# Hybrid decoder layer: block sums moved from GpSimd to VectorE, squares added by accumulating DMAs, embedding projection rounded in the last pair

## The reference

```python
h = h + y @ w_out[i]
hn = rmsnorm(h, ffn_norm_g[i])                     # D_MODEL 2048, D_FF 5632
h = h + (silu(hn @ w_gate[i]) * (hn @ w_up[i])) @ w_down[i]
e = rmsnorm(p[i] @ ple_proj[i], ple_norm_g[i])     # p: 512 x 256
gate = sigmoid(rmsnorm(h, ple_gate_norm_g[i]) @ ple_gate_w[i] + ple_gate_b[i])
h = h + gate * e
```

## Time and profile before

| | us |
|---|---|
| runs: median of 3 (lowest, highest) | 2752.56 (2748.27, 2755.18) |
| the profiled execution, its own time | 2750.89 |
| its span, first to last instruction | 2749.2 |
| PE busy | 2642.3 (96%) |
| DVE busy | 1756.5 (64%) |
| ACT busy | 1137.2 (41%) |
| POOL busy | 804.4 (29%) |

### The profile page before, as it was taken

The page is one execution under the profiler, slowest core; times in us unless marked ns, Lnnn a source line. Parts: engine busy times, 40 slices in busy tenths (PEclk is TensorE's granted clock), DMA queues, the critical chain, the costliest instruction groups (busy, mean ns, idle before and its releaser), DMA issues.

```text
span 2749.2 us, 49201 instructions
## 1 busy us (share of the span) xinstructions
PE 2642.3 (96%) x18730; PEld 2250.5 (82%) x18730; DVE 1756.5 (64%) x2078; ACT 1137.2 (41%) x1690; POOL 804.4 (29%) x672
## 2 busy tenths in 40 slices
PE   7999999999999998799999999999979999999998
PEld 6776776776776787799999999999977888888887
DVE  6654653653653535799999999999974333334443
ACT  5445535534534425444444444444433222223321
POOL 3101200210111105755555555555534000001100
PEclk9999999999999999899999999999999999999999
DMA  5222231232232334343343343344347453533532
GB/s 168 87 77 64 70 86 59 69 86 66 65 90 93 128 95 137 104 134 116 121 141 120 115 140 127 114 137 130 114 171 267 128 179 101 176 95 99 178 122 72
DMA packets 126526, 319.11 MB, mean 116 GB/s; under 512 B 37272, under 2 KB 39832, under 8 KB 126392
## 3 DMA queue, kind: packets, MB, share of 16 engines
q1 hardware_dynamic: 108096, 251.30, 29.5%
q0 software_dynamic: 18304, 66.07, 6.4%
HBM read 276.88 MB, written 40.44 MB: 115 GB/s over the span
## 4 chain that ended last, share of the span: by engine, by line
PE 37%; issue 33%; DVE 20%; POOL 5%; ACT 3%; DMA 2%; SPq 1%; DVEq 0%; POOLq 0%; ACTq 0%
PE bank L349 11%; PE bank L346 11%; PE bank L350 11%; DVE w_lo L1323 10%; DVE act_out_lo L1397 3%; DVE u_s L1417 2%; PE bank L387 1%; POOL probs L1128 1%; DVE cu L1393 1%; DVE w_lo L341 1%; DMA raw<-w_mix 1%; POOL scratch_pool L140 1%; PE bank L1355 1%; DVE cg L1412 1%; PE bank L1357 1%
## 5 line engine op out<-in xcount | busy, mean ns | idle before, releaser
L341 DVE TENSOR_TENSOR w_lo<-raw,w_hi 128x1024 fp32r<-128x1024 f32 (+2 forms) x308 | 331.5, 1079 | 424.6 <-ACT w_hi L334 423.2
L334 ACT ACTIVATE w_hi<-raw 128x1024 fp32r<-128x1024 f32 (+2 forms) x308 | 284.8, 926 | 517.1 <-PE bank L350 412.3
L346 PE MATMUL bank<-in_hi,w_hi 128*128 128x512 f32 x1088 | 457.7, 421 | 37.8 <-DVE in_lo L2002 11.4
L349 PE MATMUL bank<-in_lo,w_hi 128*128 128x512 f32 x1088 | 442.7, 407 | 0.0
L350 PE MATMUL bank<-in_hi,w_lo 128*128 128x512 f32 x1088 | 429.6, 395 | 0.0
L1355 PE MATMUL bank<-x_a,w_hi 128*128 128x256 f32 x1408 | 405.1, 288 | 24.1 <-DVE cu L1421 14.5
L1356 PE MATMUL bank<-x_a,w_hi 128*128 128x256 f32 x1408 | 400.0, 284 | 0.0
L1357 PE MATMUL bank<-x_a,w_lo 128*128 128x256 f32 x1408 | 400.0, 284 | 0.0
L1323 DVE TENSOR_TENSOR w_lo<-sum,w_hi 128x1024 fp32r<-128x1024 f32 x176 | 308.3, 1752 | 6.4 <-ACT w_hi L1318 6.3
L1355 PE MATMUL bank<-x_c,w_hi 128*128 128x256 f32 x1056 | 300.4, 284 | 7.1 <-DVE x_c L1267 4.5
L1356 PE MATMUL bank<-x_c,w_hi 128*128 128x256 f32 x1056 | 299.9, 284 | 0.0
(11 more groups left out here) (290 smaller groups left out, 5091.6 us busy)
## 6 DMA issues: line engine op xcount, KB each, us to landing
raw<-w_gu SPq DMA_DIRECT2D x154, 512.0 KB, 5.0
raw<-w_mix SPq DMA_DIRECT2D x116, 512.0 KB, 3.7
raw<-w_down SPq DMA_DIRECT2D x64, 384.0 KB, 3.1
raw<-w_down SPq DMA_DIRECT2D x64, 320.0 KB, 2.9
raw<-ple_gate SPq DMA_DIRECT2D x32, 512.0 KB, 3.6
raw_odd<-w_gu SPq DMA_DIRECT2D x22, 512.0 KB, 5.8
act_scratch<-act_out_hi POOLq DMA_DIRECT2D x44, 256.0 KB, 3.8
act_scratch<-act_out_lo POOLq DMA_DIRECT2D x44, 256.0 KB, 4.0
```

Of the source, the lines that this page charges most:

```text
L334: nc.scalar.activation(w_hi[:, ring_slots(par2, half), 0:cols[half]], raw[:, half, 0:cols[half]], ACT.Copy).then_inc(hi_ready, 1)
L341: nc.vector.tensor_tensor(w_lo[:, s, 0:cols[half]], raw[:, half, 0:cols[half]], w_hi[:, s, 0:cols[half]].bitcast(F32), ALU.subtract).then_ ...
L346: nc.tensor.matmul(out, w_h, x_hi, start=start, stop=False, skip_group_check=True)
L349: nc.tensor.matmul(out, w_h, x_lo, start=False, stop=False, skip_group_check=True)
```

## The change

The sums of weight blocks and of activation blocks are formed by DVE (`dve_sum`, `dve_x_sums`) and no longer by POOL. `hf` has three buffers in turn. The squares of the late output projection go to two buffers by parity and from there to DRAM by POOL DMAs, which after the first two add to what lies there (`accum_op`); at the end two DMAs bring the two sums back, and PE adds both in `norm_bank` before product 3 of the first pair. The fourth activation sum is cut within the first pair (`act_x6`, `dve_x6`). In the last pair ACT and DVE cut the embedding `p` and the four halves of `ple_proj` in their slots after product 3. `sq_e` has four buffers.

```diff
+    hf = [sb_at(first + k * KB, f"hf_{i}", [P, SEQ]) for i, k in enumerate((64, 154, 156))]
+    sq_h = [sb_at(first + k * KB, f"sq_h_{i}", [P, SEQ]) for i, k in enumerate((162, 164))]
...
+    def squares_added(o):
+        return S(f"moved_{o % 2}"), 16 + 16 * (o // 2 + 1)
+
+    def act_late_square(act, o):
+        if o > 1:
+            act.wait_ge(*squares_added(o - 2))
+        nc.scalar.activation(sq_h[o % 2][:], h_t[:, o, :], ACT.Square).then_inc(S("h_squared"), 1)
+
+    def pool_late_square(pool, o):
+        pool.wait_ge(S("h_squared"), o + 1)
+        if o > 1:
+            pool.wait_ge(*squares_added(o - 2))
+            pool.dma_start(squares_dram[o % 2], sq_h[o % 2][:], accum_op=ALU.add).then_inc(S(f"moved_{o % 2}"), 16)
...
     def act_x_scaled(act, o):
-        i = o // 2
         act.wait_ge(*added_late(o))
-        if i > 0:
-            act.wait_ge(S("x_summed_pool"), KT // 2 + 4 * i)
-            act.wait_ge(S("hn_ready"), 3 * i - 1)
+        if o > 2:
+            act.wait_ge(S("x_summed_dve"), KT // 2 + 4 * ((o - 1) // 2))
+            act.wait_ge(S("hn_ready"), 3 * ((o - 3) // 2) + 2)
...
     def dve_x_sums(dve, i):
+        nc.vector.tensor_tensor(t123[:, 0, :], b12, b11, ALU.subtract).then_inc(S("x_summed_dve"), 1)
+        nc.vector.tensor_tensor(t123[:, 2, :], b22, b12, ALU.subtract).then_inc(S("x_summed_dve"), 1)
+        dve.wait_ge(S("x_summed_dve"), summed(1))
+        nc.vector.tensor_tensor(t123[:, 1, :], b22, t123[:, 0, :], ALU.subtract).then_inc(S("x_summed_dve"), 1)
+        dve.wait_ge(S("x_summed_dve"), summed(3))
+        nc.vector.tensor_tensor(t4[:, i, :], b21, t123[:, 1, :], ALU.subtract).then_inc(S("x_summed_dve"), 1)
...
@@ pe_pair
-            if first and j == 2:
-                pe.wait_ge(S("h_summed"), KT + 1)
-                nc.tensor.matmul(aux[:], ones[:], acc_h[:], start=True, stop=True, skip_group_check=True
-                                 ).then_inc(S("norm_summed"), 1)
+            if first and j == 3:
+                for half in range(2):
+                    pe.wait_ge(S(f"moved_{half}"), SQUARES_BACK)
+                    last = nc.tensor.matmul(norm_bank[:], ones[:], sq_h[half][:], start=half == 0, stop=half == 1,
+                                            skip_group_check=True)
+                last.then_inc(S("norm_summed"), 1)
@@ act_pair
+            if first and j == 1:
+                act_x6(act)
+            if first and j == 3:
+                rstd_of(act, rstd_h, NORM_FFN, norm_bank)
...
+            if last and j == 3:
+                for k in range(2):
+                    nc.scalar.activation(p_hi[:, k, :], p_raw[:, k, :], ACT.Copy).then_inc(S("act_hi_ready"), 1)
+            if last and j >= 3:
+                round_slab(act, N_PROJ + (j - 3) // 2, (j - 3) // 2, halves=((j - 3) % 2,), unloaded=UNLOADED)
@@ dve_pair
+            if j == 0:
+                dve_sum(dve, p, q, 4)
+            if j in (2, 3) and not last:
+                dve_sum(dve, p + 1, (q + 1) % QUAD, j - 1)
...
                 nc.vector.tensor_tensor(cu[:, right], u5_s[:], d, ALU.add).then_inc(combined, 1)
+                if not last:
+                    dve_sum(dve, p + 1, (q + 1) % QUAD, 3)
...
+            if first and j == 3:
+                dve_x6(dve)
+            if last and j == 3:
+                for k in range(2):
+                    dve.wait_ge(S("act_hi_ready"), PAIRS + k)
+                    nc.vector.tensor_tensor(p_lo[:, k, :], p_raw[:, k, :], p_hi[:, k, :].bitcast(F32), ALU.subtract
+                                            ).then_inc(S("low_part_ready"), 1)
+            if last and j >= 3:
+                subtract_slab(dve, N_PROJ + (j - 3) // 2, (j - 3) // 2, halves=((j - 3) % 2,))
@@ SP, after the last pair's loads
-            sp.wait_ge(lo_ready, blocks(PRODUCTS * (PAIRS - 1) + 2))
+            sp.dma_start(raw[:, 0, :], d["ple_proj"][0][:, first_half]).then_inc(raw_landed[0], 16)
             sp.wait_ge(sum_ready, 4 * PAIRS)
-            for u in range(PROJ_SLABS):
+            sp.dma_start(raw[:, 1, :], d["ple_proj"][0][:, second_half]).then_inc(raw_landed[1], 16)
+            for u in range(1, PROJ_SLABS):
                 load_slab(sp, N_PROJ + u, d["ple_proj"][u])
@@ PE, embedding projection
-            pe.wait_ge(S("low_part_ready"), PAIRS + 2)
+            pe.wait_ge(S("low_part_ready"), PAIRS + 1)
...
-                        pe.wait_ge(copied, 3 * PAIRS)
-                    elif t == 1:
-                        pe.wait_ge(combined, 7 * (PAIRS - 1) + 1)
-                    else:
+                        pe.wait_ge(copied, 3 * (PAIRS - 1))
+                        pe.wait_ge(combined, 7 * (PAIRS - 1))
+                    elif t > 1:
                         pe.wait_ge(tile_evacuated, TILE_PROJ + t - 1)
@@ POOL, end of the pairs
             load_act(0)
+            pool_store_act(pool, PAIRS - 1)
             pool.wait_ge(lo_ready, blocks(PRODUCTS * PAIRS))
             for i in range(2):
                 load_residual(i)
-            pool_store_act(pool, PAIRS - 1)
```

More of the change, by code:

```diff
@@ L78 @@
 TILE_GATE = TILE_DOWN + CHUNKS * OUT_SLABS
+SQUARES_BACK = 16 + 16 * (KT // 2 + 1)
 DOWN_CUT_AT = (5, 8, 13)
@@ L214, in layer @@
     e_t = sb_at(first, "e_t", [P, KT, SEQ])
-    sq_e = sb_at(first + 44 * KB, "sq_e", [P, 2, SEQ])
+    sq_e = [sb_at(first + k * KB, f"sq_e_{i}", [P, SEQ]) for i, k in enumerate((44, 46, 52, 54))]
     acc_e = sb_at(first + 48 * KB, "acc_e", [P, SEQ])
@@ L1254, in act_x_scaled @@
                              ).then_inc(S("hn_hi_ready"), 1)
     def act_x_blocks(act, i):
+        even, odd = hf[2 * i % 3], hf[(2 * i + 1) % 3]
         act.wait_ge(S("hn_hi_ready"), 2 * i + 2)
-        nc.scalar.activation(x_hi[0][:, i, :], hf[:, 0, 0:TH], ACT.Copy).then_inc(S("in_hi_ready"), 1)
-        nc.scalar.activation(x_c[:, 0:2, i, :], by_half(hf[:, 1, :]), ACT.Copy).then_inc(S("in_hi_ready"), 1)
+        nc.scalar.activation(x_hi[0][:, i, :], even[:, 0:TH], ACT.Copy).then_inc(S("in_hi_ready"), 1)
@@ L1303, in layer @@
     blocks = lambda count: 2 * N_FFN + count
-    gu_banks = lambda q: [psum[(4 if q % 2 == 0 else 0) + i] for i in range(4)]
+    gu_banks = lambda q: [psum[4 * (q % 2) + i] for i in range(4)]
     gu_slot = lambda q, j: (PRODUCTS * q + j) % RING
@@ L1336, in pe_pair @@
                 pe.wait_ge(combined, 7 * p - 7)
+            if j == 0 and isinstance(p, int) and p == 1:
+                pe.wait_ge(S("norm_logged"), NORM_FFN)
+            if first and j == 1:
+                pe.wait_ge(*added_late(OUT_SLABS - 1))
             if j == 3:
@@ L1371, in act_pair @@
                 act_copy_product(act, p, q, j)
-            if first and j == 2:
-                rstd_of(act, rstd_h, NORM_FFN)
+            if first and j == 1:
+                act_x6(act)
+            if first and j == 3:
+                rstd_of(act, rstd_h, NORM_FFN, norm_bank)
             if j == 6:
@@ L1438, in pool_sums, with dve_sum @@
+            if last and j >= 3:
+                subtract_slab(dve, N_PROJ + (j - 3) // 2, (j - 3) // 2, halves=((j - 3) % 2,))
+    def dve_sum(dve, p, q, k):
         s1, s2, s3, s4 = (t[:] for t in sums)
         a11, a12, a21, a22 = raw_11[q % 2], raw_12, raw_21[:], raw_22[q % 2][:]
-        had_one = not (isinstance(p, int) and p == 0)
-        s_count = lambda k: 4 * p + k
-        if 1 in which:
-            pool.wait_ge(*landing("21", p, q))
-            pool.wait_ge(*landing("22", p, q))
-            if had_one:
-                pool.wait_ge(lo_ready, blocks(PRODUCTS * p - 4))
-            nc.gpsimd.tensor_tensor(s1, a21, a22, ALU.add).then_inc(sum_ready, 1)
@@ L1459, in pool_sums @@
-        pool.wait_ge(sum_ready, s_count(2))
-        if had_one:
-            pool.wait_ge(lo_ready, blocks(PRODUCTS * p - 1))
-        nc.gpsimd.tensor_tensor(s4, a12, s2, ALU.subtract).then_inc(sum_ready, 1)
+        if not (isinstance(p, int) and p == 0):
+            dve.wait_ge(lo_ready, blocks(PRODUCTS * p - 5 + k))
+        if k == 1:
+            dve.wait_ge(*landing("21", p, q))
+            dve.wait_ge(*landing("22", p, q))
+            nc.vector.tensor_tensor(s1, a21, a22, ALU.add).then_inc(sum_ready, 1)
@@ new lines, in dve_sum @@
+        if k == 2:
+            dve.wait_ge(*landing("11", p, q))
+            dve.wait_ge(sum_ready, 4 * p + 1)
+            nc.vector.tensor_tensor(s2, s1, a11, ALU.subtract).then_inc(sum_ready, 1)
+        if k == 3:
+            nc.vector.tensor_tensor(s3, a11, a21, ALU.subtract).then_inc(sum_ready, 1)
+        if k == 4:
+            dve.wait_ge(*landing("12", p, q))
+            dve.wait_ge(sum_ready, 4 * p + 2)
+            nc.vector.tensor_tensor(s4, a12, s2, ALU.subtract).then_inc(sum_ready, 1)
@@ L1955, in _ @@
                     act.wait_ge(tile_evacuated, TILE_PROJ + t + 1)
-                    after(act, S("e_summed"), t - 1)
-                    nc.scalar.activation(sq_e[:, t % 2, :], e_t[:, t, :], ACT.Square).then_inc(S("e_squared"), 1)
```

(2 more changed lines are left out.)

168 lines of the change are left out of this document (75 added, 93 removed).

## The result

The changed kernel takes 2708.94 us (median of 4 runs, 2706.22 to 2709.99) against 2751.88 us (4 runs, 2748.27 to 2755.18): a ratio of 0.9843, 95% interval 0.9826 to 0.986, so 43 us or 1.6% faster. The forecast was 2694 with a range of 2681 to 2718. The profiled execution took 2708.09 us, its span 2706.4 us.

A forecast was written before the change was run, and what follows sets the result against it. PE was taken to set the pairs' pace, with DVE's fullness being hold-ups by POOL's reads; gains 24.9 + 6.1 + 12.8 + 14.4 = 58.2 us from 2750.9 gave 2692.7, median 2694 us, range 2681 to 2718.

The forecast's parts named there:

- the loop: Steady pairs: PE's gap of 0.59 us before product 6 goes in 42 pairs, 24.9 us gained.
- the late projection: Late output projection: six periods of two tiles fall from 8.12 to 6.7 us; 6.1 us gained in all.
- the first pair: Last residual addition to pair 1: 29.5 us in place of 42.3, 12.8 us gained.
- the end: Behind the last pair: embedding's last tile 27 us after the last product in place of 41.4, 14.4 us gained.
- VectorE becomes the bound: Rival, pairs: DVE's 199 us are work, sums come on top, about 2920 us; chance 0.05, shared with other losses.
- some 6.4 us with the overlap of neighbours, and I take 6.7: Late output projection: DVE's ten operations per two tiles take 6.4 us, 6.7 with two short waits for ACT.
- the cycle is then 6.8 and just hidden: Late output projection: with the accumulating DMA at 6 us, the squares' cycle per parity is 6.8 us and hidden.
- ACT waiting for no squares: Sign in the profile after: in the late output projection, two tiles in 6.7 us and no ACT wait for squares.
- The squares are slow: Rival, late output projection: accumulating DMAs take 9.7 us, cycle 10.5, time 2721 us; chance 0.13.
- last square X + 2.4: First pair: the last square is done 2.4 us after the last residual addition X.
- cuts the fourth activation sum (half of 4.45...): First pair: DVE's cut of the fourth activation sum takes half of 4.45 us, as nothing holds it up.
- 24 in all, done at 31.3, before PE comes to `acc_e`: End: POOL's squares, 1.51 us each, finish 31.3 us after the last product, before PE needs `acc_e` at about 33.8.

The follow-up runs named there:

- run 1: Changed kernel plus four POOL additions of 128x512 per pair in 40 pairs, reading SBUF, nobody waiting for them: 2707.86 us.
- run 2: Changed kernel plus four POOL memsets of 128x512 per pair in 40 pairs, each behind a single-column addition: 2706.52 us.
- run 3: Changed kernel plus eight POOL additions of 128x512 per pair in 40 pairs, reading SBUF, nobody waiting for them: 2802.5 us.
- run 10: Changed kernel with squares added on POOL in SBUF and the end as before, leaving only the block sums on DVE: 2717.37 us.
- run 4: Changed kernel with plain stores in place of the 14 accumulating DMAs of the squares: 2703.11 us.
- run 9: Changed kernel with the second residual load behind POOL's eighth addition into `acc_e` and x6 ahead of the block subtraction in the first pair: 2694.04 us.
- run 7: Changed kernel with the second residual load at the end issued by POOL behind the eighth of its sixteen additions into `acc_e`: 2700.19 us.
- run 5: Changed kernel with the squares of the late output projection added by POOL in SBUF as before: 2712.63 us.
- run 8: Changed kernel with x6 worked out ahead of the block subtraction in the first pair: 2703.9 us.
- run 11: Changed kernel with x6 ahead of the block subtraction in the first pair and the second residual load issued by SyncE, not POOL: 2695.14 us.
- run 6: Changed kernel with the end as before: `p` and first `ple_proj` slabs rounded behind the last pair, residual loads ahead of the last stores: 2710.34 us.

## Why the prediction was right, and where it was off

**Verdict and mechanism: right.** By the stretches 42.8 us were gained where the sum had 58.2: 24.5 for 24.9 in the loop, 6.3 for 6.1 in the late projection, 8.5 for 12.8 in the first pair and 3.5 for 14.4 at the end. DVE's fullness was being held up by POOL's reads. Runs 1 to 3 show this from the other side: reads put the stretches back, writes don't, and with a dose that exceeds DVE's slack PE waits before product 6 again. Run 10, with the sums alone on DVE, has the whole 24.9 us in the pairs. The rival *VectorE becomes the bound* fell with 172.80 of 200 us.

**The loop: right.** 24.5 us against 24.9, a sum at 1.22 against 1.21, 17.4 us of DVE per pair against 18.2. The missing 0.8 is the overlap of neighbours, which the sum of single durations doesn't have: the groups of 1200 to 1900 us still add up to 18.3 us per pair.

**The late output projection: the sum was right by two errors.** "some 6.4 us with the overlap of neighbours, and I take 6.7" was too long: free of POOL the period is 5.61. It counted the two cuts of `x_c` at 0.69 and 1.21 us, the second from the earlier trace rows, and both were themselves held up; they take 0.42 and 0.69, and these 0.79 us are the whole way from 6.4 to 5.61. "the cycle is then 6.8 and just hidden" failed for the same reason: the transfers landed in the 6 us I took (median 6.2), but 6.8 hides behind 6.7 and not behind 5.61. ACT waits 12.8 us there, three of the six periods are 7.3 to 9.2 us, and the mean, 6.81 over six periods, is near my 6.7 by accident. The sign "ACT waiting for no squares" thus failed. The rival *The squares are slow* is real in kind and smaller than its price: without the adding the kernel is 5.8 us faster (run 4), where the rival had 27.

**The first pair: the term was mis-sized**, 8.5 for 12.8. "last square X + 2.4" came at X + 7.5, as two more squares stood 1.0 and 2.6 us for their buffers, in front of the last blocks' rounding in ACT's queue; PE waited 3.0 us for `x_c`, 1.4 for `w_lo` and 1.2 for the squares' way back, and product 3 ended near X + 20, not X + 16. Behind it the forecast held: "cuts the fourth activation sum (half of 4.45...)" was right in size (2.28), product 6 opened 9.4 us after product 3's end where I had 9.2, and it took 4.0 where I had 4.3. So the 4.3 us lie ahead of product 3's end, for the most part in the squares' delay. That is read from the trace and not tested piece by piece. What I had on the path behind product 3, and took as given, could be shortened: run 9 takes 3.4 us off there.

**The end: the step "24 in all, done at 31.3, before PE comes to `acc_e`" failed.** An addition takes the 1.5 to 1.6 us of the earlier trace rows, but the sixteen began 16.8 us after the last product's end and not near 7, as "done at 31.3" implies, because I put the DMAs ahead of them in POOL's order at nothing. The sequencer stood 6.77 us before the second residual load; run 7 moved that load and brought 8.8 us. With the additions in time the rest of the term holds: the embedding's last tile 27.6 us after the last product, where I had 27. The fourth half of `ple_proj` was not late, and PE's wait after tile 1 was 4.11 us, where I had about 4. The trace of before had a stop of the same kind, 3.38 us of "issue" in POOL until 2049.39, between its residual loads and the last stores. DVE's low part, for which these stores wait as well, was done at 2046.70, so some 2.7 us of it are the stop. I read that stretch for PE, ACT and DVE only.

**What stays open.** What exactly POOL's sequencer stands for. The traces narrow it down. In the changed kernel and in runs 1 to 5 and 8 the stop comes before the eighth DMA from the first load of `act` on, and it ends 1.33 us after the second of these loads has landed, each time. In the changed kernel that load is the row below, issued at 2002.67 (KB, us to landing):

```profile
act_lo<-act_scratch POOLq DMA_DIRECT2D x1, 1536.0 KB, 15.5
```

It landed at 2018.22, and the residual load followed at 2019.55. In runs 7, 9 and 11 the eighth DMA comes when that load has landed long before, and the stop is 1.34 to 1.36 us. So the 6.77 us are read best as a wait for an old transfer and a fixed 1.33 us behind it; no run tested this by itself. With the end as before (the kernel before and runs 6 and 10) the stop comes before the seventh DMA and does not fit the 1.33 us: in run 6 the store went 1.6 us after its low part was ready, ahead of any landing of the four loads. More than two buffers for the late squares weren't tried, as SBUF is full there.

## What to carry to other kernels

A duration in a stretch where GpSimd reads SBUF is not the instruction's own; look for the same shape where GpSimd is quiet before adding up VectorE's work or a period, and use it for every term, also for the period that something else is meant to hide behind. When work is taken off a saturated engine, the next limit is whatever was "just hidden" by the old pace. Large DMAs in an engine's order aren't free for the instructions behind them: put a load that isn't needed soon behind the chain that somebody waits for. And a wait of TensorE can cost more than its own length, when the granted clock falls behind it.
